# Last expert pair by column blocks with an early scatter, and filler products ahead of the mask

## The chip, the cores and the metric

The kernel runs on one core of a Trainium2 chip. The metric is the device time of one execution in microseconds. One program computes the whole model; no collective is in it.

## The reference

A trunk of two residual layers on 256 tokens of width 2048, all float32. Layer 0 mixes tokens with a chunkwise mLSTM, layer 1 with latent attention (MLA). Behind each mixer stands a mixture of 16 experts in 4 groups, of which each token uses 2:

```python
for i in range(DEPTH):
    x = x + mixer_i(rmsnorm(x, norm_mix[i]))
    x = x + moe_ffn(rmsnorm(x, norm_ffn[i]), router_w, router_b, w_gate[i], w_up[i], w_down[i])

def moe_ffn(xn, ...):
    scores = sigmoid(xt @ router_w); sel = scores + router_b
    # best group of 4 experts, its best 2, their scores normalised to gates
    hg, hu = xt @ w_gate[e], xt @ w_up[e]          # 2048 -> 512 for each expert e
    a = silu(hg) * hu * gates
    y = sum over e of a[e] @ w_down[e]             # 512 -> 2048
```

An expert's three matrices have 12 MB, so those of a layer are 192 units of 1 MB. Each is read once.

## The kernel before

The order of the work is written out by hand for each engine, with semaphores between them. The program in order of time: mLSTM projections and heads with its output projection (to about 437 us), router, experts of layer 0 (to about 910), MLA (to about 1273), router, experts of layer 1.

**Loads.** SP issues all weight loads. In an expert stage a load is mostly a double unit of 2 MB into one of 8 double slots (DOUBLE, OVD, WIDED), and it waits (`room`) until PE has used what lay there, counted by the semaphore `unit_used`. The down weights' last two double units of the last pair (`HALVES = 4`) come as four loads of 1 MB, first the two first halves (k = 0, experts e = 0 and 1), then the two second halves (L489).

**Start of an expert stage.** PE ends the router's logits (L657), VectorE and ScalarE make from them a mask of the two experts of each token (L1771 to L1795), and PE waits for it in `route` (L836): three products (L837 to L839) give each token its position in its expert's list of up to 64 tokens, two (L841, L842) the counts. VectorE makes a selection matrix (L1823), and `gather` (L868) takes the normalised tokens XN, which ScalarE writes meanwhile in eight pieces (L1322), to the experts' slots in four column groups. The first pair gathers two groups, multiplies with the first half of the weights (L908), gathers two more and goes on.

**A pair** (function `pair` of PE) handles two experts side by side in the two halves of TensorE's columns, 64 slots each: gate and up products (L908), in whose gaps the scatter of the pair before stands; transposes of A and of the selection (L922 to L927); the down products (L940). These run over c, the four blocks of the contraction (512 = 4 x 128), and inside it over d, the four column blocks of the result, which lie in PSUM banks 4 to 7. Blocks c = 0 and 1 need the first double unit of down weights of each expert, c = 2 and 3 the second; in the last pair c = 2 needs the first halves and c = 3 the second halves of it. After c = 3, d each column block is read by ScalarE (Y_hi, L1338) and by VectorE (Y_lo, L1873).

**Scatter and add.** `scatter` (L880, L881) brings column block d of the two experts' results back to the two token blocks t, two products for each, into banks 2 and 3. `add_block` of VectorE (L1837) adds them to X. The scatter of block d + 1 waits until the add of block d has read its bank. Behind the last pair of a layer the four scatters stand behind all down products, and VectorE's four `add_block` behind all four Y_lo (semaphore `x_final`).

**Behind layer 0** `turn_final` (L599) transposes each finished column block for the attention layer, VectorE multiplies it with the norm's gains (`final_turned`, L1520), ScalarE (L1308) and POOL (L566) split it into a high and a low part, and PE's first attention products (`token_unit`, L627) need these and the high (ScalarE, L1149) and the low part (VectorE, L1510) of the weights. Behind layer 1 SP stores each column block of X (L540).

Of the kernel before, what the change touches and what calls it, by code (L numbers as in the profile page):

```python
# [136 lines left out]
TURNS = ("h", "n2")  # L137
N2_BANKS = (0, 4, 6, 2)

# [38 lines left out]
def trunk(nc, w, out):  # L178
# [8 lines left out]
    with ctx:  # L187
# [405 lines left out]
        def _(pe):  # L593
# [256 lines left out]
            def experts(l, base):  # L850
# [21 lines left out]
                def scatter(m, j, d, final=False):  # L872

                    pe.wait_ge(sem(m + "y_low"), 4 * j + d + 1)
                    for t in range(NT):
                        if d > 0 and final:
                            pe.wait_ge(sem("x_final"), 8 * l + 2 * d + t - 1)
                        elif d > 0:
                            pe.wait_ge(sem(m + "x_added"), 8 * (j - l) + 2 * d + t - 1)
                        pe.matmul(PS[:, 2 + t, :], SCT[:, t * P:(t + 1) * P], YH[:, d, :], start=True, stop=False)  # L880
                        pe.matmul(PS[:, 2 + t, :], SCT[:, t * P:(t + 1) * P], YL[:, d, :], start=False, stop=True)\  # L881
                            .then_inc(sem(m + "scattered"), 1)

                def pair(m, j, g, following, arrived, slot, consumed, whole, prev, first=False):
# [46 lines left out]

                    for c in range(FC):
                        units = [16 + 4 * (c // 2) + 2 * e + c % 2 for e in range(2)]
                        for n in units:
                            arrived(n)
                        for d in range(4):
                            if c == 0 and d == 2:
                                pe.wait_ge(sem(m + "sct_ready"), j + 1)
                            for e in range(2):
                                last = pe.matmul(PS[64 * e:64 * e + 64, 4 + d, :], m_["AT"][:, c, 64 * e:64 * e + 64],  # L940
                                                 slot(units[e])[:, d, :], start=(c == 0), stop=(c == FC - 1))
                                if d == 3:
                                    finished(last, units[e])
# [52 lines left out]
            for n in range(4):  # L996
                token_unit(S_CKV + n, (0, 1), XTP, UNIT_K * n, n == 0, n == 3, False, chunks("n2", n), True)
                if n < 2:
                    turn_final(n + 2)
            pe.wait_ge(sem("few_lo"), 2)  # L1000
            for k in range(DC):
                last = three(PS[0:ROPE, 4, 0:SEQ], [v[:, k, :] for v in WKRP], (XTH[:, k, :], XTL[:, k, :]),
                             k == 0, k == DC - 1)
# [68 lines left out]
            for i in range(N_PAIR):  # L1072
# [6 lines left out]
                if i == 0:  # L1079
                    pe.wait_ge(sem("krope_copied"), 1)  # L1080
                    for t in range(NT):
                        last = pe.transpose(PS[:, 4, t * ROPE:(t + 1) * ROPE], KRX[:, t * P:(t + 1) * P],
                                            IDENT[0:ROPE, 0:ROPE])
# [49 lines left out]
        def _(act):  # L1133
# [246 lines left out]
            for t in range(NT):  # L1380
                act.activation(b_["CKV"][:, t, :], PS[:, t, :], ACT.Copy, scale=RST[:, t:t + 1]).then_inc(sem("ckv_copied"), 1)
            high(S_PAIRS + 1)
            act.wait_ge(sem("krope_done"), 1)
            act.activation(KRX, PS[0:ROPE, 4, 0:SEQ], ACT.Copy).then_inc(sem("krope_copied"), 1)
            act.wait_ge(sem("ckv_means"), 1)
            act.activation(SSQ[:, 4:6], SSQ[:, 2:4], ACT.Sqrt).then_inc(sem("ckv_roots"), 1)
            act.wait_ge(sem("krope_done"), 2)
            for t in range(NT):
                last = act.activation(b_["KR"][:, t, :], PS[:, 4, t * ROPE:(t + 1) * ROPE], ACT.Copy, scale=RST[:, t:t + 1])
            last.then_inc(sem("krope_copied"), 1)  # L1390
# [104 lines left out]
        def _(dve):  # L1495
# [319 lines left out]
            def experts(l):  # L1815
# [17 lines left out]
                def add_block(m, j, d, counted):  # L1833
                    for t in range(NT):
                        dve.wait_ge(sem(m + "scattered"), 8 * j + 2 * d + t + 1)
                        xs = X[:, t, d * UNIT_C:(d + 1) * UNIT_C]
                        tt(xs, PS[:, 2 + t, :], xs, ALU.add).then_inc(sem(counted), 1)  # L1837

# [10 lines left out]

                def pair(m, j, following, ahead, products, prev, i, first):  # L1850
                    select_again(m, j, i, first)
# [31 lines left out]
                def main(i, j, following, ahead, prev):  # L1883
                    pair(m, j, following, lambda: ahead, lambda n: dve.wait_ge(sem("unit_used"), base + PAIR_UNITS * i + n), prev, i, 0)

# [259 lines left out]
```

## Time and profile before

| | |
|---|---|
| median of 3 runs | 1754.29 us (1751.32 to 1754.47) |
| the profiled execution | 1753.88 us |
| its span | 1752.1 us, mean granted clock 0.99 |
| PE busy | 1689.9 us (96%) |
| VectorE, ScalarE, POOL busy | 756.4, 493.7, 51.8 us |
| DMA | 531.70 MB, 303 GB/s over the span |

A profile comes from one execution. Times in it are in microseconds from the span's start. "Idle before" is the time for which an engine did nothing ahead of an instruction, with what ended it. PEclk is the granted clock of TensorE as a share of 2.4 GHz, so 0.50 is 1.2 GHz. The chain of waits is followed back from the last instruction. An f32 product stands in it as two records. The DMA share is that of the core's 16 DMA engines.

### The profile page before, as it was taken

To read this page: it belongs to the slowest core of one execution; us is meant where nothing else is said; L and a number is where in the kernel's file an instruction comes from. 1 tells how busy PE (TensorE), PEld (TensorE's weight loads), DVE (VectorE), ACT (ScalarE), POOL (GpSimd) and SP (SyncE) were. 2 spreads that over 40 slices of the span, in tenths; PEclk is the share of its full clock that TensorE was granted. 3 is DMA by queue.
4 is the path that set the end of the run, shared out by engine and by line. 5 is a ranking of instruction groups with operands and counts; after the bars stand their busy time and mean duration, and the time that the engine had idled before them with its cause. 6 is when DMAs were issued, how large, how long until landed. Compare 5 with 4: busy or idle time off the path is not lost.

```text
span 1752.1 us, 21040 instructions
## 1 busy us (share of the span) xinstructions
PE 1689.9 (96%) x8834; PEld 1095.5 (63%) x8834; DVE 756.4 (43%) x1276; ACT 493.7 (28%) x649; POOL 51.8 (3%) x32
## 2 busy tenths in 40 slices
PE   7999999999899999999999999999989999999998
PEld 7998777788444443443458999988854443444343
DVE  4775577754222222222246777784422222222222
ACT  4435456542200000000034565664330000000000
POOL 2000000000000000000021000010000000000000
PEclk9999999999899999999999999999989999999999
DMA  9655534464999999999994545454589999999996
GB/s 312 204 184 168 188 123 129 136 211 149 380 420 428 427 428 428 427 427 428 427 373 156 161 133 156 145 173 161 195 341 420 428 428 428 426 428 428 426 428 280
DMA packets 102376, 531.70 MB, mean 303 GB/s; under 512 B 11764, under 2 KB 28680, under 8 KB 76936
## 3 DMA queue, kind: packets, MB, share of 16 engines
q1 hardware_dynamic: 101904, 530.16, 77.0%
q8 instruction: 74, 1.21, 0.3%
q10 hardware_dynamic: 344, 0.13, 0.0%
q14 instruction: 22, 0.18, 0.0%
q0 software_dynamic: 32, 0.02, 0.0%
HBM read 528.19 MB, written 2.10 MB: 303 GB/s over the span
## 4 chain that ended last, share of the span: by engine, by line
PE 85%; DMA 10%; DVE 2%; ACT 1%; issue 1%; ACTq 0%; DVEq 0%; SPq 0%
PE PS L627 31%; PE PS L908 19%; PE PS L940 13%; PE PS L868 7%; PE PS L710 5%; DMA DOUBLE<-in_moe_w_up 5%; DMA OVD<-in_moe_w_up 3%; DMA OVD<-in_moe_w_down 2%; PE PS L880 2%; PE PS L881 1%; PE PS L795 1%; PE PS L1043 1%; PE PS L1069 1%; PE PS L657 1%; ACT AREA L1330 1%
## 5 line engine op out<-in xcount | busy, mean ns | idle before, releaser
L908 PE MATMUL PS<-DOUBLE,AREA 128*64 128x512 f32 x1280 | 350.0, 604 | 22.1 <-DMA DOUBLE<-in_moe_w_up 8.2
L1510 DVE TENSOR_TENSOR LO<-ring,HI 128x2048 fp32r<-128x2048 f32 (+1 forms) x124 | 267.2, 2155 | 182.0 <-ACT HI L1149 181.8
L1149 ACT ACTIVATE HI<-ring 128x2048 fp32r<-128x2048 f32 (+1 forms) x124 | 223.7, 1805 | 275.6 <-PE PS L627 228.5
L908 PEld LDWEIGHTS PS<-DOUBLE,AREA 128*64 128x64 f32 x1280 | 107.5, 139 | 236.4 <-issue 228.9
L908 PE MATMUL PS<-OVD,AREA 128*64 128x512 f32 x512 | 229.6, 596 | 0.0
L1837 DVE TENSOR_TENSOR X<-PS,X 128x512 f32<-128x512 f32 x128 | 82.4, 686 | 331.1 <-PE PS L881 331.1
L940 PE MATMUL PS<-DOUBLE,AREA 128*64 128x512 f32 x640 | 168.2, 594 | 2.1 <-DMA OVD<-in_moe_w_down 0.2
L627 PE MATMUL PS<-HI,XTH 128*128 128x512 f32 (+1 forms) x672 | 159.7, 379 | 1.5 <-ACT HI L1149 1.5
L627 PE MATMUL PS<-LO,XTH 128*128 128x512 f32 (+1 forms) x672 | 152.8, 369 | 0.0
L627 PE MATMUL PS<-HI,XTL 128*128 128x512 f32 (+1 forms) x672 | 152.5, 368 | 0.0
L627 PEld LDWEIGHTS PS<-HI,XTL 128*128 128x128 f32 x672 | 122.9, 188 | 16.4
L627 PEld LDWEIGHTS PS<-LO,XTH 128*128 128x128 f32 x672 | 122.8, 188 | 16.5 <-DVE LO L1510 0.3
L627 PEld LDWEIGHTS PS<-HI,XTH 128*128 128x128 f32 x672 | 121.0, 188 | 18.6 <-ACT HI L1149 2.1
L868 PEld LDWEIGHTS PS<-AREA,XN 128*128 128x128 f32 x1024 | 121.3, 199 | 13.9 <-issue 13.0
L1873 DVE SCALAR_TENSOR_TENSOR Y_lo<-PS,AREA,Y_hi 128x512 fp32r<-128x512 f32 x64 | 48.1, 751 | 189.4 <-ACT Y_hi L1338 183.8
L868 PE MATMUL PS<-AREA,XN 128*128 128x128 f32 x1024 | 124.7, 284 | 0.8 <-DVE AREA L1823 0.8
L1328 ACT ACTIVATE AREA<-PS 128x512 f32<-128x512 f32 x16 | 9.6, 597 | 410.7 <-PE PS L908 410.7
L908 PE MATMUL PS<-WIDED,AREA 128*64 128x512 f32 x256 | 115.6, 595 | 5.5 <-DMA OVD<-in_moe_w_up 5.5
L940 PEld LDWEIGHTS PS<-DOUBLE,AREA 128*64 128x64 f32 x640 | 52.9, 137 | 103.6 <-issue 100.1
L940 PE MATMUL PS<-OVD,AREA 128*64 128x512 f32 x256 | 111.7, 594 | 0.0
L1338 ACT ACTIVATE Y_hi<-PS,AREA 128x512 fp32r<-128x512 f32 x64 | 44.0, 688 | 192.5 <-PE PS L940 192.5
L1846 DVE TENSOR_TENSOR AREA<-PS,VFF 128x512 f32<-128x512 f32 x64 | 44.3, 692 | 102.0 <-PE PS L868 102.0
(291 smaller groups left out, 1828.8 us busy)
## 6 DMA issues: line engine op xcount, KB each, us to landing
DOUBLE<-in_moe_w_gate SPq DMA_DIRECT2D x48, 2048.0 KB, 20.4
DOUBLE<-in_moe_w_down SPq DMA_DIRECT2D x40, 2048.0 KB, 21.8
DOUBLE<-in_moe_w_up SPq DMA_DIRECT2D x32, 2048.0 KB, 23.3
ring<-in_a_w_in SPq DMA_DIRECT2D x48, 1024.0 KB, 5.1
OVD<-in_moe_w_gate SPq DMA_DIRECT2D x16, 2048.0 KB, 24.8
WIDED<-in_moe_w_up SPq DMA_DIRECT2D x16, 2048.0 KB, 22.5
OVD<-in_moe_w_up SPq DMA_DIRECT2D x16, 2048.0 KB, 27.1
OVD<-in_moe_w_down SPq DMA_DIRECT2D x14, 2048.0 KB, 27.3
```

What stands on the lines that cost most here:

```text
L627: mm = pe.matmul(PS[:, banks[t], 0:n], lhs(k0 + kk, t)[part], weights[:, kk, 0:n], start=first and kk == 0 and p == 0, stop=last and kk == ...
L710: last = pe.matmul(PS[:, 4 * (b % 2) + ch, 0:SEQ], weights[:, kk, ch * P:(ch + 1) * P], tokens[:, k, :], start=k == 0 and p == 0, stop=k = ...
L868: last = pe.matmul(PS[:, bank, k * P:(k + 1) * P], XN[:, t, c * P:(c + 1) * P], m_["SEL"][:, t, :], start=(t == 0), stop=(t == NT - 1))
L880: pe.matmul(PS[:, 2 + t, :], SCT[:, t * P:(t + 1) * P], YH[:, d, :], start=True, stop=False)
L908: last = pe.matmul(PS[64 * e:64 * e + 64, up, :], m_["XG"][:, c, 64 * e:64 * e + 64], slot(units[e])[:, kk, :], start=(c == 0), stop=(c == ...
L940: last = pe.matmul(PS[64 * e:64 * e + 64, 4 + d, :], m_["AT"][:, c, 64 * e:64 * e + 64], slot(units[e])[:, d, :], start=(c == 0), stop=(c ...
L1149: act.activation(HI[s % 2][:, :, 0:n], ring[PLACE[u]][:, :, 0:n], ACT.Copy).then_inc(sem("hi_ready"), 1)
L1338: act.activation(YH[:, d, :], PS[:, 4 + d, :], ACT.Copy, scale=m_["GS"])\
L1510: tt(LO[PLACE[u]][:, :, 0:n], ring[PLACE[u]][:, :, 0:n], HI[s % 2][:, :, 0:n], ALU.subtract)\
L1837: tt(xs, PS[:, 2 + t, :], xs, ALU.add).then_inc(sem(counted), 1)
L1846: tt(m_["XG"][:, 4 * g:4 * g + 4, :], ps4(2 + g % 2), VFF[:, l, 4 * g:4 * g + 4].unsqueeze(2).broadcast_to([P, 4, P]), ALU.mult)\
L1873: stt(YL[:, d, :], PS[:, 4 + d, :], m_["GS"], YH[:, d, :], ALU.mult, ALU.subtract)\
```

## The change

1. `route` of both layers begins with four f32 products of 512 columns (ONES by X) into bank 0, ahead of the wait for the mask. Nobody reads their result.
2. In the last pair of each layer the down products of c = 0 and 1 stand as before. Those of c = 2 and 3 go by column block: both for d = 0, both for d = 1, and so on. The waits for the first and second halves of the last double units stand together ahead of them.
3. Scatter of column block 0 stands between the down products of d = 2 and d = 3, and VectorE's add of block 0 ahead of its Y_lo 3.
4. The final scatters use banks 2 and 3 for d = 0 and 2, and banks 0 and 1 for d = 1 and 3 (`FINAL_BANKS`); block d waits for the adds of block d - 2.
5. `turn_final` uses banks 4, 6, 2, 0 in this order (before 0, 4, 6, 2), the first attention unit's results go to banks 4 and 5 (before 0 and 1), and the rope part of the keys to bank 0 (before 4).

```diff
+            def keep_on(bank, *columns):
+                for n in columns:
+                    pe.matmul(PS[:, bank, 0:n], ONES, X[:, 0, 0:n], start=True, stop=True)
+
             def route(l):
+                keep_on(0, 512, 512, 512, 512)
                 pe.wait_ge(sem("mask_ready"), l + 1)
...
                     for t in range(NT):
-                        if d > 0 and final:
-                            pe.wait_ge(sem("x_final"), 8 * l + 2 * d + t - 1)
-                        elif d > 0:
+                        bank = FINAL_BANKS[d] + t if final else 2 + t
+                        if d > 1 and final:
+                            pe.wait_ge(sem("x_final"), 8 * l + 2 * d + t - 3)
+                        elif d > 0 and not final:
                             pe.wait_ge(sem(m + "x_added"), 8 * (j - l) + 2 * d + t - 1)
...
+                    ending = whole and not following
+                    for c in range(2 if ending else FC):
+                        down_arrived(c)
                         for d in range(4):
                             if c == 0 and d == 2:
                                 pe.wait_ge(sem(m + "sct_ready"), j + 1)
+                            last = down(c, d)
                             if c == FC - 1 and d < 3:
                                 last.then_inc(sem(m + "y_done"), 1)
+                    if ending:
+                        down_arrived(2)
+                        down_arrived(3)
+                        for d in range(4):
+                            down(2, d)
+                            last = down(3, d)
+                            if d < 3:
+                                last.then_inc(sem(m + "y_done"), 1)
+                            if d == 2:
+                                scatter(m, j, 0, True)
...
-                for d in range(4):
+                for d in range(1, 4):
                     scatter(m, pair_turn(l, PAIRS - 1), d, True)
...
                     for d in range(4):
+                        if d == 3 and last_one:
+                            add_block(m, j, 0, "x_final")
                         dve.wait_ge(sem(m + "y_ready"), 4 * j + d + 1)
...
-                for d in range(4):
+                for d in range(1, 4):
                     add_block(m, pair_turn(l, PAIRS - 1), d, "x_final")
```

PE ahead of the mask products, first the kernel before, then the changed one (L657 and L658 are the logits, MK is the mask, the words in brackets are the semaphores waited for):

```order
L657 MATMUL PS<-RW,XT_110 128x16 [waits x_columns]
L657 MATMUL PS<-RW,XT_110 128x16 x3
L837 MATMUL PS<-MK,TRI_R 128x16 [waits mask_ready]
L838 MATMUL PS<-MK,ONE_R 128x16
L839 MATMUL PS<-MK,TRI_R 128x16
```

```order
L658 MATMUL PS<-RW,XT_110 128x16 [waits x_columns]
L658 MATMUL PS<-RW,XT_110 128x16 x3
L839 MATMUL PS<-X,CON 128x512 x4
L845 MATMUL PS<-MK,TRI_R 128x16 [waits mask_ready]
L846 MATMUL PS<-MK,ONE_R 128x16
L847 MATMUL PS<-MK,TRI_R 128x16
```

The four filler products (CON holds ONES) stand between the logits and the wait for the mask.

PE at the end of layer 1, the second half of the down products. Before, its first rows and those where c = 3 begins (unit_loaded_12 and 14 are the first halves, 13 and 15 the second halves):

```order
L940 MATMUL PS<-DOUBLE_111,AREA 64x512
L940 MATMUL PS<-OVD_60,AREA 64x512
L940 MATMUL PS<-WIDED,AREA 64x512 [waits unit_loaded_14,unit_loaded_12]
L940 MATMUL PS<-OVD_59,AREA 64x512
L940 MATMUL PS<-WIDED,AREA 64x512
L940 MATMUL PS<-OVD_59,AREA 64x512
L940 MATMUL PS<-WIDED,AREA 64x512
L940 MATMUL PS<-OVD_59,AREA 64x512
L940 MATMUL PS<-WIDED,AREA 64x512
L940 MATMUL PS<-OVD_59,AREA 64x512
L940 MATMUL PS<-WIDED,AREA 64x512 [waits unit_loaded_15,unit_loaded_13]
L940 MATMUL PS<-OVD_59,AREA 64x512
```

The changed kernel at the same place:

```order
L944 MATMUL PS<-DOUBLE_111,AREA 64x512
L944 MATMUL PS<-OVD_60,AREA 64x512
L944 MATMUL PS<-WIDED,AREA 64x512 [waits unit_loaded_13,unit_loaded_15,unit_loaded_14,unit_loaded_12]
L944 MATMUL PS<-OVD_59,AREA 64x512
L944 MATMUL PS<-WIDED,AREA 64x512
L944 MATMUL PS<-OVD_59,AREA 64x512
```

Before, the second halves are waited for eight rows (four column blocks) later than the first halves; now all four loads are waited for ahead of the first product of the second half.

VectorE at the end of layer 1, before and now:

```order
L1870 CAST SCT<-PS 128x256
L1873 SCALAR_TENSOR_TENSOR Y_lo<-PS,AREA,Y_hi 128x512 [waits m_y_ready] x4
L1837 TENSOR_TENSOR X<-PS,X 128x512 [waits m_scattered] x8
```

```order
L1898 CAST SCT<-PS 128x256
L1903 SCALAR_TENSOR_TENSOR Y_lo<-PS,AREA,Y_hi 128x512 [waits m_y_ready] x3
L1865 TENSOR_TENSOR X<-PS,X 128x512 [waits m_scattered] x2
L1903 SCALAR_TENSOR_TENSOR Y_lo<-PS,AREA,Y_hi 128x512 [waits m_y_ready]
L1865 TENSOR_TENSOR X<-PS,X 128x512 [waits m_scattered] x6
```

Two of the eight adds now stand ahead of the last Y_lo.

## Rows read from the trace of the kernel before

**Rows 1.** Busy time by stretch: us, each engine's busy us (x), PEclk, DMA share, GB/s.

```profile
672.00:889.00 217.00, 203.03 (x1006) 87.54 (x1002) 51.70 (x88) 14.23 (x23) 0.00 (x0) 0.99 1.01 427
911.00:1268.00 357.00, 354.59 (x1913) 316.44 (x1911) 240.68 (x406) 193.18 (x279) 28.10 (x11) 1.00 0.51 166
```

**Rows 2.** The chain that ended last, layer 1's end: start us, us, what.

```profile
1688.15 27.87 DMA DOUBLE<-in_moe_w_up
...
1716.15 8.75 PE PS L908 x32
...
1727.47 14.00 PE PS L940 x64
...
1742.22 0.75 DVE Y_lo L1873
```

**Rows 3.** Timeline of VectorE, the last two adds: start us, us, what, [idle before].

```profile
1747.61 1.29 DVE L1837 TENSOR_TENSOR X<-PS,X 128x512 f32<-128x512 f32 x2 [0.29 <-PE PS L881]
```

**Rows 4.** Start of both expert stages: PE and ScalarE timelines, then the chain.

```profile
445.70 0.38 PE L837 MATMUL PS<-MK,TRI_R 128*128 128x16 f32 x1 [4.08 <-DVE MK L1795]
...
442.69 9.13 ACT L1322 ACTIVATE XN<-X,SSQ 128x512 f32<-128x512 f32 x8
...
1281.82 0.38 PE L837 MATMUL PS<-MK,TRI_R 128*128 128x16 f32 x1 [4.40 <-DVE MK L1795]
...
447.32 6.59 PE PS L868 x32
453.91 13.88 PE PS L908 x64
467.79 3.77 PE PS L868 x32
...
1283.44 6.66 PE PS L868 x32
```

**Rows 5.** Busy time by stretch, the clock at layer 0's start.

```profile
444.00:452.00 8.00, 5.91 (x27) 5.82 (x28) 3.70 (x17) 7.82 (x7) 0.00 (x0) 0.50 1.00 429
454.00:456.00 2.00, 2.00 (x10) 0.61 (x10) 0.64 (x1) 0.00 (x0) 0.00 (x0) 1.00 0.99 410
```

**Rows 6.** Busy time by stretch, where the load slots are full.

```profile
458.00:464.00 6.00, 6.00 (x30) 2.01 (x28) 0.00 (x0) 0.00 (x0) 0.00 (x0) 1.00 0.63 208
1294.00:1300.00 6.00, 6.00 (x32) 2.00 (x30) 0.00 (x0) 0.00 (x0) 0.00 (x0) 1.00 0.54 180
```

**Rows 7.** The last half loads (L489), SP's timeline and times to landing, both layers.

```profile
869.80 0.43 SPq L489 DMA_DIRECT2D OVD<-in_moe_w_down  x1
...
DMA to landing us min/median/max: 23.3/26.7/30.0
...
1705.41 0.43 SPq L489 DMA_DIRECT2D OVD<-in_moe_w_down  x1
...
DMA to landing us min/median/max: 24.2/27.3/30.3
```

**Rows 8.** The chain: a scatter between two groups of products.

```profile
512.42 7.02 PE PS L908 x32
...
519.87 0.23 PE PS L881
...
520.56 7.02 PE PS L908 x32
```

**Rows 9.** End of layer 0: the chain, then VectorE's timeline.

```profile
889.48 14.11 PE PS L940 x64
...
910.17 2.48 DVE L1510 TENSOR_TENSOR LO<-ring,HI 128x2048 fp32r<-128x2048 f32 x1
```

**Rows 10.** PE timeline: products behind an idle time, with the idle time before them.

```profile
794.46 5.33 PE L908 MATMUL PS<-DOUBLE,AREA 128*64 128x512 f32 x16 [2.57 <-DVEq L1906]
...
869.88 3.65 PE L908 MATMUL PS<-DOUBLE,AREA 128*64 128x512 f32 x16 [1.42 <-DMA DOUBLE<-in_moe_w_gate]
...
1716.15 2.83 PE L908 MATMUL PS<-DOUBLE,AREA 128*64 128x512 f32 x6 [2.28 <-DMA DOUBLE<-in_moe_w_up]
```

More of the change, by code:

```diff
@@ L137 @@
 TURNS = ("h", "n2")
-N2_BANKS = (0, 4, 6, 2)
+N2_BANKS = (4, 6, 2, 0)
+FINAL_BANKS = (2, 0, 2, 0)
 OVER_PE = (("gathered", 4 * OVER_PAIRS + 4), ("a_turned", OVER_PAIRS), ("sel_turned", OVER_PAIRS), ("y_done", 3 * OVER_PAIRS),
@@ L875, in scatter @@
                     for t in range(NT):
-                        if d > 0 and final:
-                            pe.wait_ge(sem("x_final"), 8 * l + 2 * d + t - 1)
-                        elif d > 0:
+                        bank = FINAL_BANKS[d] + t if final else 2 + t
+                        if d > 1 and final:
+                            pe.wait_ge(sem("x_final"), 8 * l + 2 * d + t - 3)
+                        elif d > 0 and not final:
                             pe.wait_ge(sem(m + "x_added"), 8 * (j - l) + 2 * d + t - 1)
-                        pe.matmul(PS[:, 2 + t, :], SCT[:, t * P:(t + 1) * P], YH[:, d, :], start=True, stop=False)
-                        pe.matmul(PS[:, 2 + t, :], SCT[:, t * P:(t + 1) * P], YL[:, d, :], start=False, stop=True)\
+                        pe.matmul(PS[:, bank, :], SCT[:, t * P:(t + 1) * P], YH[:, d, :], start=True, stop=False)
+                        pe.matmul(PS[:, bank, :], SCT[:, t * P:(t + 1) * P], YL[:, d, :], start=False, stop=True)\
                             .then_inc(sem(m + "scattered"), 1)
@@ L930, in pair, with down, down_arrived @@
                     pe.wait_ge(sem(m + "at_ready"), j + 1)
-                    for c in range(FC):
+                    def down(c, d):
                         units = [16 + 4 * (c // 2) + 2 * e + c % 2 for e in range(2)]
-                        for n in units:
-                            arrived(n)
+                        for e in range(2):
+                            last = pe.matmul(PS[64 * e:64 * e + 64, 4 + d, :], m_["AT"][:, c, 64 * e:64 * e + 64],
+                                             slot(units[e])[:, d, :], start=(c == 0), stop=(c == FC - 1))
+                            if d == 3:
+                                finished(last, units[e])
+                        return last
+                    def down_arrived(c):
+                        for e in range(2):
+                            arrived(16 + 4 * (c // 2) + 2 * e + c % 2)
+                    ending = whole and not following
+                    for c in range(2 if ending else FC):
+                        down_arrived(c)
                         for d in range(4):
@@ L938, in pair @@
                                 pe.wait_ge(sem(m + "sct_ready"), j + 1)
[L939 to L943, printed above, removed]
+                            last = down(c, d)
                             if c == FC - 1 and d < 3:
                                 last.then_inc(sem(m + "y_done"), 1)
+                    if ending:
[8 more added lines that the diff above has]
+                                scatter(m, j, 0, True)
                     if following:
@@ L996, in _ @@
             for n in range(4):
-                token_unit(S_CKV + n, (0, 1), XTP, UNIT_K * n, n == 0, n == 3, False, chunks("n2", n), True)
+                token_unit(S_CKV + n, (4, 5), XTP, UNIT_K * n, n == 0, n == 3, False, chunks("n2", n), True)
                 if n < 2:
@@ L1001, in _ @@
             for k in range(DC):
-                last = three(PS[0:ROPE, 4, 0:SEQ], [v[:, k, :] for v in WKRP], (XTH[:, k, :], XTL[:, k, :]),
+                last = three(PS[0:ROPE, 0, 0:SEQ], [v[:, k, :] for v in WKRP], (XTH[:, k, :], XTL[:, k, :]),
                              k == 0, k == DC - 1)
@@ L1081, in _ @@
                     for t in range(NT):
-                        last = pe.transpose(PS[:, 4, t * ROPE:(t + 1) * ROPE], KRX[:, t * P:(t + 1) * P],
+                        last = pe.transpose(PS[:, 0, t * ROPE:(t + 1) * ROPE], KRX[:, t * P:(t + 1) * P],
                                             IDENT[0:ROPE, 0:ROPE])
@@ L1380, in _ @@
             for t in range(NT):
-                act.activation(b_["CKV"][:, t, :], PS[:, t, :], ACT.Copy, scale=RST[:, t:t + 1]).then_inc(sem("ckv_copied"), 1)
+                act.activation(b_["CKV"][:, t, :], PS[:, 4 + t, :], ACT.Copy, scale=RST[:, t:t + 1]).then_inc(sem("ckv_copied"), 1)
             high(S_PAIRS + 1)
             act.wait_ge(sem("krope_done"), 1)
-            act.activation(KRX, PS[0:ROPE, 4, 0:SEQ], ACT.Copy).then_inc(sem("krope_copied"), 1)
+            act.activation(KRX, PS[0:ROPE, 0, 0:SEQ], ACT.Copy).then_inc(sem("krope_copied"), 1)
             act.wait_ge(sem("ckv_means"), 1)
@@ L1388, in _ @@
             for t in range(NT):
-                last = act.activation(b_["KR"][:, t, :], PS[:, 4, t * ROPE:(t + 1) * ROPE], ACT.Copy, scale=RST[:, t:t + 1])
+                last = act.activation(b_["KR"][:, t, :], PS[:, 0, t * ROPE:(t + 1) * ROPE], ACT.Copy, scale=RST[:, t:t + 1])
             last.then_inc(sem("krope_copied"), 1)
@@ L1836, in add_block @@
                         xs = X[:, t, d * UNIT_C:(d + 1) * UNIT_C]
-                        tt(xs, PS[:, 2 + t, :], xs, ALU.add).then_inc(sem(counted), 1)
+                        bank = FINAL_BANKS[d] + t if counted == "x_final" else 2 + t
+                        tt(xs, PS[:, bank, :], xs, ALU.add).then_inc(sem(counted), 1)
                 def added(m, j):
@@ L1848, in gathered, with pair @@
                             .then_inc(sem(m + "xg_ready"), 1)
-                def pair(m, j, following, ahead, products, prev, i, first):
+                def pair(m, j, following, ahead, products, prev, i, first, last_one=False):
                     select_again(m, j, i, first)
@@ L1883, in main @@
                 def main(i, j, following, ahead, prev):
-                    pair(m, j, following, lambda: ahead, lambda n: dve.wait_ge(sem("unit_used"), base + PAIR_UNITS * i + n), prev, i, 0)
+                    pair(m, j, following, lambda: ahead, lambda n: dve.wait_ge(sem("unit_used"), base + PAIR_UNITS * i + n), prev, i, 0, not following)
                 main(0, pair_turn(l, 0), True, gather_turn(l, 1), False)
```

## Prediction

> **What bounds the kernel now.** The profiled execution took 1753.88 us with a span of 1752.1; the median of the runs shown is 1754.29, 0.4 us above it. The sum below is made against the profiled one; about 0.2% (3.5 us) is what a measurement of this kernel can tell from no change.
>
> I read the stretches first [rows 1]. In the second half of each expert stage the DMA engines are fully busy at 427 GB/s while PE has some 14 us of idle in 217. So weights streaming in set the end of both expert stages, and PE only adds what it does after the last weights. In the attention stage between them PE is busy 354.6 of 357 us: a delay handed to it passes through.
>
> Next the chain that ended last, at the end of layer 1 [rows 2]: it comes from a landing (the last up weights, until 1716.02), then 8.75 us of products, the 14.00 us of down products, a Y_hi and a Y_lo of 1.5 us together (to 1742.97). Behind it two adds to X at a time take 1.29 us and are preceded by 0.29 us of waiting for a scatter, a period of 1.57, until 1748.90 [rows 3]: scatter and add take turns on one pair of banks. The store follows.
>
> Then the start of an expert stage [rows 4]. PE is idle 4.08 us (layer 0) and 4.40 us (layer 1) for the mask. The granted clock is 0.50, that is 1.2 GHz, from 444 to 452 and back at 2.4 GHz at 454 [rows 5]. The first 32 gather products therefore take 6.59 and 6.66 us where the same number takes 3.77 at full clock: 2.8 and 2.9 us. This would be hidden behind the DMA, but the slots are full at that point: the next load is issued when PE has finished with the first double slot, and for six us DMA moves 208 and 180 GB/s in place of 427 [rows 6]. That is (427 - 208) x 6 / 427 = 3.1 us of lost streaming in layer 0 and 3.5 in layer 1, which a DMA-bound stage never gets back.
>
> **Part 1: four filler products, twice.** Each is an f32 product of 512 columns. The nearest row is 64 records (32 half-width products, 16 pairs side by side) in 13.88 us: 0.87 us each; from the 128-column gather (3.77 us for 16 products, times four for the columns) it would be 0.94. Four take 3.5 to 3.8 us at full clock. They start when the logits end (445.70 - 4.08 = 441.62; in layer 1 1281.82 - 4.40 = 1277.42) and end at 445.1 to 445.4 and 1280.9 to 1281.2, ahead of the mask products (445.70, 1281.82) [rows 4]. Queued behind them on PE are only those mask products. The gather then runs at full clock, if these products keep it granted or bring it back before 447.3. It is not limited elsewhere at once: ScalarE writes XN in eight pieces of 1.14 us from 442.69 [rows 4], so the second column group, after four of them, is ready at 447.3, as the first group starts.
>
> PE gains 2.8 and 2.9 us there. The next load is issued that much sooner, and the stream, which lost 3.1 and 3.5, gains at most 2.9. Bounds: nothing to 2.9 in each layer. I take 2.5 and 2.7, since a load's rate also rises only over some 2 us after an idle queue. **-5.2 us.**
>
> **Part 2: the second half of the down products in column blocks.** The first half takes 8 of 16 steps of 14.00 / 16 = 0.875 us, so 7.0 us. Before, the third quarter waited for the first two half loads and the fourth for the last two. Now both waits stand ahead of the first column block, after 7.0 us in place of 10.5. The last half load was issued at 869.80 and 1705.41 and took 30.0 and 30.3 us: it lands at 899.8 and 1735.7 [rows 7]. DMA sets this, so it moves with part 1 but not with part 2.
>
> Layer 1: down starts at 1727.47, the first half ends at 1734.5, PE waits 1.3 us, restarts at about 1735.9. Then 7.0 us of products and one scatter between them. Between products a scatter costs what lies from 512.42 + 7.02 = 519.44 to 520.56, 1.12 us [rows 8]. The last product ends at 1744.0 (1741.5 before). Y_hi and Y_lo take 1.5 us (to 1745.5). Block 0 is then already added, in the time VectorE waits for the last Y_hi, and with two pairs of banks the other three blocks run at VectorE's own 1.29 us: 1749.4 against 1748.9 (1747.61 + 1.29) [rows 3]. So +0.5, and +0.1 as the stores, 1.57 us apart before, come 1.29 apart: **+0.6 us.** Without the wait it would be 0.9 us faster: from the last product to the last add 7.4 us fall to 5.4, less 1.1 for the scatter.
>
> By the Trainium skill, "TensorEngine Tiling (Array Packing)", Key Properties, a change of tiling mode drains TensorE. The scatter is full width and stands between half-width products, so it changes mode twice. By the rate of scatter products in a row (0.23 [rows 8]) the term would be 0.93, by the row with both changes in it 1.12, which stands in the sum; the rule costs 0.2 us per layer and the trace agrees with it.
>
> Layer 0: down starts at 889.48, the first half ends at 896.5, the last half load lands at 899.8. PE waits **3.4 us**. Then 8.1 us: 908.1 in place of 889.48 + 14.11 = 903.6 [rows 9]. Y_lo 3 ends at 909.6. VectorE then does three double operations (add 1, the turned block, add 2) where it did four: 3 x 1.28, so the low half of the first attention weights starts at 913.4 in place of 910.17 [rows 9]. PE's second group of attention products needs that low half. **+3.2 us**, and PE, busy through the attention stage [rows 1], absorbs none of it.
>
> The clock after that wait: an idle time of 2.57 us ahead of 794.46 was followed by slow products, 16 records in 5.33 us in place of 3.65 [rows 10]: **+1.7 us.** Bounds: nothing to 1.7. I take 1.7, since 3.4 us is longer than that row's idle time.
>
> The new PSUM banks move no work; the attention stage's waits for them are for operations that it waited for anyway. I cost them at nothing.
>
> Sum: 1753.88 - 5.2 + 3.2 + 1.7 + 0.6 = **1754.2 us**: what the fillers give is spent on the wait for the last loads in layer 0. Chance 0.42.
>
> **Rivals.**
> (a) The wait is there, the clock stays: 1.7 less, **1752.5**, 0.2. For it: an idle time of 1.42 us ahead of 869.88 left the clock alone (the 16 records behind it took 3.65) [rows 10]. Against it: 2.28 us ahead of 1716.15 did not, and the 32 records there took 8.75 in place of 7.02 [rows 2, 8]. Where the limit falls isn't seen. The Trainium skill, "TensorE: Matmul & The Clock Gate", Part 1, says that the monitor behind the clock runs free of the program; by it the same wait may cost nothing in one run and 1.7 in the next, and no run so far shows this wait twice.
> (b) Layer 0's delay is absorbed in the attention stage, where ScalarE and VectorE have waits of their own: -5.2 + 0.6, **1749.3**, 0.15. Against it: PE's 354.6 of 357 us.
> (c) Slower: the fillers themselves run at 1.2 GHz. Ahead of them PE has had little but the router's 16-column products, and the clock was down by 444 [rows 5]. Four fillers then take 7 us, end at 448.6 and 1284.4, and hold back the mask products by 2.9 and 2.5. The gather still gains its 2.8, so the fillers gain 0 and 0.3: 1753.88 - 0.3 + 5.5 = **1759.1**, 0.15. It decides from the point where the fillers end more than some 2 us after the mask; half of them cold ends 1 us late and only costs 1 us of the gain.
> (d) The change doesn't do what it says: the fillers leave the clock at half in the gather too. They are then 2.9 and 2.5 us late for nothing: 1753.88 + 5.4 + 5.5 = **1764.8**, 0.03.
> The last 0.05 is for what I have not thought of.
>
> **How the numbers follow.** Faster needs 1750.8 or less: (b), and a little of (a): 0.19. Slower needs 1757.8: (c) and (d): 0.18. Within: 0.63. The range takes in the forecast with its bounds (gains of 4.5 to 5.7 in part 1, 0 to 1.7 of clock), most of (a), and the nearer half of (b) and (c): 1749.8 to 1757.8.
>
> **What would show it.** First gather products near 3.8 us in both layers and the clock at 1.0 at 446:448; the load after them issued 2.8 us sooner relative to the mask. In layer 0 a PE wait of about 3.4 us for a down load, followed by products at half clock; in layer 1 one of about 1.3. X adds of blocks 1 to 3 without gaps of 0.28 between them. From the first gather product to the last down landing some 2.5 us less. If PE has no wait for the last loads, the steps of part 2 are wrong, and the time is 1 us better in layer 1 and over 3 in layer 0; if fillers end after the mask, (c) is at work.

## The result, and the profile of the changed kernel

| | before | changed |
|---|---|---|
| median of 20 runs | 1752.36 us (1749.13 to 1754.51) | 1756.1 us (1752.7 to 1759.46) |
| ratio | | 1.0021, 95% interval 1.0014 to 1.0028 |
| profiled execution | 1753.88 us | 1757.23 us |
| its span | 1752.1 us | 1755.6 us, mean granted clock 0.994 |
| PE busy | 1689.9 us | 1694.0 us |
| VectorE, ScalarE, POOL busy | 756.4, 493.7, 51.8 us | 756.1, 493.2, 51.8 us |

The changed kernel is slower by 3.7 us (2.5 to 4.9). The forecast was no change. The time, 1756.1, lies in the range, but the median of before fell to 1752.36 with more runs: the profile against which the sum was made was 1.5 us above it.

The start of the expert stages first. PE's timeline of the changed kernel, both layers (start us, us, instructions, idle before with what ended it):

```profile
441.38 3.68 PE L839 MATMUL PS<-X,CON 128*128 128x512 f32 x8
445.62 0.28 PE L845 MATMUL PS<-MK,TRI_R 128*128 128x16 f32 x1 [0.55 <-DVE MK L1822]
447.18 3.84 PE L876 MATMUL PS<-AREA,XN 128*128 128x128 f32 x32 [0.84 <-DVE AREA L1850]
...
1279.43 3.68 PE L839 MATMUL PS<-X,CON 128*128 128x512 f32 x8
1283.98 0.28 PE L845 MATMUL PS<-MK,TRI_R 128*128 128x16 f32 x1 [0.87 <-DVE MK L1822]
1285.55 5.46 PE L876 MATMUL PS<-AREA,XN 128*128 128x128 f32 x32 [0.84 <-DVE AREA L1850]
```

The four fillers take 3.68 us and end 0.55 and 0.87 us ahead of the mask, at full clock. In layer 0 the gather takes 3.84 us where it took 6.59 [rows 4]. In layer 1 it takes 5.46 (6.66 before): 1.2 us less and not 2.8, so more than half of what the fillers should give is missing. The stretches agree (each engine's busy us, PEclk, DMA share, GB/s):

```profile
458.00:464.00 6.00, 6.00 (x32) 2.00 (x30) 0.00 (x0) 0.00 (x0) 0.00 (x0) 1.00 0.95 363
1284.00:1290.00 6.00, 5.16 (x30) 5.07 (x31) 2.25 (x9) 6.00 (x6) 0.00 (x0) 0.72 1.01 434
1294.00:1300.00 6.00, 6.00 (x30) 2.01 (x28) 0.00 (x0) 0.00 (x0) 0.00 (x0) 1.00 0.84 303
```

Where the load slots are full, DMA moved 208 and 180 GB/s [rows 6]; now it moves 363 and 303. The second of these stretches does not stand at the same place of its stage, since the mask of layer 1 comes 2.16 us later. Over sixty us at the same place (from 440 in layer 0, from 1277 before and 1279.16 now in layer 1) the rate rises from 403 to 417 GB/s in layer 0, and from 404 to 412 in layer 1. The granted clock of 1284 to 1290 is 0.72: it is 1.00 until 1285 and 0.50 from 1286 to 1289, so most of that gather ran at 1.2 GHz.

Then the last pair. PE's timeline shows three idle times: ahead of the second half of the down products in each layer, and in the middle layer 1's last up products.

```profile
896.96 1.08 PE L944 MATMUL PS<-WIDED,AREA 128*64 128x512 f32 x1 [2.88 <-DMA OVD<-in_moe_w_down]
...
1717.40 7.09 PE L917 MATMUL PS<-DOUBLE,AREA 128*64 128x512 f32 x32 [2.33 <-DMA DOUBLE<-in_moe_w_up]
...
1737.07 1.09 PE L944 MATMUL PS<-WIDED,AREA 128*64 128x512 f32 x1 [2.80 <-DMA OVD<-in_moe_w_down]
```

PE waits 2.88 and 2.80 us for a down load. In the kernel before, its longest wait for one in these two pairs was 0.25 us. The first record behind the wait takes 1.08 us, where the first one of the down products, at full clock, takes 0.61, and the stretches show the clock:

```profile
897.00:900.00 3.00, 3.00 (x8) 1.07 (x10) 0.00 (x0) 0.00 (x0) 0.00 (x0) 0.50 1.05 386
...
1737.00:1738.00 1.00, 0.93 (x4) 0.37 (x6) 0.00 (x0) 0.00 (x0) 0.00 (x0) 0.50 0.00 0
```

The chain of waits tells what each layer's end hangs on. Layer 0:

```profile
869.00 27.83 DMA OVD<-in_moe_w_down
...
896.96 6.97 PE PS L944 x24
...
905.06 1.92 PE PS L944 x8
...
907.73 0.75 DVE Y_lo L1903
908.48 1.20 DVE X L1865 x2
909.67 1.20 DVE AREA L1547 x2
910.87 1.20 DVE X L1865 x2
912.06 2.70 DVE LO L1537
...
914.81 3.97 PE PS L628 x16
```

Layer 1:

```profile
1706.62 30.32 DMA OVD<-in_moe_w_down
...
1737.07 6.75 PE PS L944 x24
...
1744.94 1.92 PE PS L944 x8
...
1747.61 0.75 DVE Y_lo L1903
1748.36 2.39 DVE X L1865 x4
...
1751.35 0.60 DVE X L1865
```

Both now begin with the landing of the last half load. Where the 3.5 us of span come from:

- Layer 0: PE's first products with the low half of the attention weights start at 914.81, before at 912.71: +2.1. This passes through the attention stage whole: the mask of layer 1 comes at 1283.98, before at 1281.82 [rows 4], +2.16.
- Layer 1, from mask to last add: 1751.95 - 1283.98 = 467.97; before 1748.90 - 1281.82 = 467.08: +0.9.
- From the last add to the end of the span: 3.65 us, before 3.2: +0.45.

### The profile page after: what moved, and what is told of

Same layout as the page of the kernel before. It is cut to its first block, busy times and chain, and to the rows that moved or that the text cites. A ratio compares the mean times of both kernels' runs of the same rounds, so it can differ in the third digit from the quotient of the medians.

```text
span 1755.6 us, 21070 instructions
## 1 busy us (share of the span) xinstructions
PE 1694.0 (96%) x8850; PEld 1094.4 (62%) x8850; DVE 756.1 (43%) x1276; ACT 493.2 (28%) x649; POOL 51.8 (3%) x32
## 4 chain that ended last, share of the span: by engine, by line
PE 79%; DMA 16%; DVE 2%; ACT 1%; issue 1%; SPq 0%; ACTq 0%; DVEq 0%
PE PS L628 30%; PE PS L917 15%; PE PS L944 11%; DMA OVD<-in_moe_w_up 6%; PE PS L876 6%; DMA DOUBLE<-in_moe_w_up 6%; PE PS L711 5%; DMA OVD<-in_moe_w_down 3%; PE PS L889 1%; PE PS L796 1%; PE PS L890 1%; PE PS L1070 1%; PE PS L1096 1%; PE PS L658 1%; PE PS L1075 0%
## 5 line engine op out<-in xcount | busy, mean ns | idle before, releaser
L917 PE MATMUL PS<-OVD,AREA 128*64 128x512 f32 x512 | 229.8, 596 | 0.0
L628 PE MATMUL PS<-HI,XTH 128*128 128x512 f32 (+1 forms) x672 | 159.9, 379 | 1.8 <-ACT HI L1176 1.5
L628 PE MATMUL PS<-LO,XTH 128*128 128x512 f32 (+1 forms) x672 | 152.8, 369 | 0.8 <-DVE LO L1537 0.8
L628 PE MATMUL PS<-HI,XTL 128*128 128x512 f32 (+1 forms) x672 | 152.5, 368 | 0.0
L628 PEld LDWEIGHTS PS<-LO,XTH 128*128 128x128 f32 x672 | 122.8, 188 | 17.5 <-DVE LO L1537 1.3
L628 PEld LDWEIGHTS PS<-HI,XTL 128*128 128x128 f32 x672 | 122.9, 188 | 16.4
L628 PEld LDWEIGHTS PS<-HI,XTH 128*128 128x128 f32 x672 | 120.9, 188 | 19.2 <-ACT HI L1176 2.1
L876 PEld LDWEIGHTS PS<-AREA,XN 128*128 128x128 f32 x1024 | 117.3, 194 | 14.8 <-issue 13.0
L876 PE MATMUL PS<-AREA,XN 128*128 128x128 f32 x1024 | 120.7, 279 | 1.7 <-DVE AREA L1850 1.7
L944 PE MATMUL PS<-OVD,AREA 128*64 128x512 f32 x256 | 115.4, 607 | 0.0
```

The lines of the kernel that those rows point to most:

```text
L628: mm = pe.matmul(PS[:, banks[t], 0:n], lhs(k0 + kk, t)[part], weights[:, kk, 0:n], start=first and kk == 0 and p == 0, stop=last and kk == ...
L876: last = pe.matmul(PS[:, bank, k * P:(k + 1) * P], XN[:, t, c * P:(c + 1) * P], m_["SEL"][:, t, :], start=(t == 0), stop=(t == NT - 1))
L917: last = pe.matmul(PS[64 * e:64 * e + 64, up, :], m_["XG"][:, c, 64 * e:64 * e + 64], slot(units[e])[:, kk, :], start=(c == 0), stop=(c == ...
```

## The experiments

Two names for short: the "early wait" is that both pairs of half loads are waited for ahead of the second half; the "exit" of layer 1 is the time from the first down product of the last pair to the end of the last add. It was 1748.90 - 1727.47 = 21.43 us before and is 1751.95 - 1727.19 = 24.76 in the changed kernel. For layer 0 the same is counted to the first low products (L627, L628): 23.23 and 27.81. All medians below stand beside runs of the kernel before on the same chip.

### 1. Each half of the change alone

The fillers alone:

```diff
 def route(l):
+    keep_on(0, 512, 512, 512, 512)
     pe.wait_ge(sem("mask_ready"), l + 1)
```

> The kernel before with the four filler products in both layers and nothing else. Theory A (the slowdown is all in the last pair; the fillers gain 2.9 us where the clock is up for the gather and 1.2 where it falls between mask and gather, as in layer 1 of the changed kernel's trace): 1.2 to 5.8 us under before, likeliest 4, and both ends of the expert stages as before, with no wait for a half load. Rival B (the fillers do not shorten the stage, the DMA gives nothing back): within 1 us of before. Rival C (the fillers cost, the ending is innocent): 2 us or more over before.

Measured: 1748.0 us against 1752.22, ratio 0.9978 (0.9969 to 0.9987): **4.2 us faster**. Both gathers run at full clock, in PE's timeline:

```profile
447.17 3.84 PE L872 MATMUL PS<-AREA,XN 128*128 128x128 f32 x32 [0.84 <-DVE AREA L1827]
...
1280.96 3.84 PE L872 MATMUL PS<-AREA,XN 128*128 128x128 f32 x32 [0.59 <-DVE AREA L1827]
```

PE saves 2.8 us in each. From gather to first down product layer 0 takes 886.97 - 447.17 = 439.80 us, before 889.48 - 447.32 = 442.16: 2.4 less. Layer 1, from gather to the last up products, takes 1.9 less (430.85 and 432.71). Rivals B and C fall.

In layer 1 the fillers of this run did not stay at full clock themselves. PE's timeline and the stretch show it:

```profile
1274.53 5.38 PE L836 MATMUL PS<-X,CON 128*128 128x512 f32 x8
...
1276.00:1278.00 2.00, 2.00 (x3) 0.72 (x3) 1.50 (x7) 2.00 (x4) 0.00 (x0) 0.50 0.97 418
```

They took 5.38 us in place of 3.68, and the gather started 6.43 us after the first of them, where it is 6.12 in the changed kernel's layer 1: 0.3 us of the gain is lost. This is rival (c) of the prediction in its half form.

The rest of the change, without fillers:

> The changed kernel without its fillers. Theory A: the early wait for the last half loads costs about 3 us of idle PE and 1.5 of slow clock in layer 0 and 1.5 to 4 in layer 1, so 6 to 9 us over before, PE idle ahead of the second half of the down products 3.4 us in layer 0. Rival B (fillers worth nothing): 3 to 4 over before, as the changed kernel. Rival C: no slower than before.

Measured: 1759.05 us, ratio 1.0041 (1.0027 to 1.0054): **6.8 us slower**. Its idle times:

```profile
899.50 0.69 PE L943 MATMUL PS<-WIDED,AREA 128*64 128x512 f32 x1 [3.31 <-DMA OVD<-in_moe_w_down]
...
1740.97 0.61 PE L943 MATMUL PS<-WIDED,AREA 128*64 128x512 f32 x1 [2.77 <-DMA OVD<-in_moe_w_down]
```

So the change is two of opposite sign, and the second is the larger: -4.2 + 6.8 = +2.6, against +3.7 measured for both, within what the intervals allow.

### 2. Is it the wait, or what came with it?

The early wait alone, in the kernel before: no fillers, column blocks or new banks.

```diff
 for c in range(FC):
     units = [16 + 4 * (c // 2) + 2 * e + c % 2 for e in range(2)]
-    for n in units:
+    early = whole and not following
+    for n in [] if early and c == 3 else units + [20 + 2 * e + 1 for e in range(2)] if early and c == 2 else units:
         arrived(n)
```

> The kernel before with one thing changed: in the last pair of each layer the wait for the second half loads stands ahead of c = 2 in place of c = 3. No fillers, no column blocks, no new banks. Theory A (the wait alone makes the slowdown): PE idle 3 to 3.4 us ahead of c = 2 in layer 0 and 1.3 to 2.8 in layer 1, mostly with slow products behind, 5 to 8 us over before. Rival (the wait needs the column blocks or the scatter to cost): under 3 us over before.

Measured: 1759.4 us against 1751.93, ratio 1.0041 (1.0027 to 1.0054): **7.5 us slower**, as much as the whole second part. In each layer the two second half loads, waited for eight products (3.5 us) sooner, make the slowdown:

```profile
898.23 0.81 PE L941 MATMUL PS<-WIDED,AREA 128*64 128x512 f32 x1 [4.04 <-DMA OVD<-in_moe_w_down]
...
1738.41 1.08 PE L941 MATMUL PS<-WIDED,AREA 128*64 128x512 f32 x1 [2.80 <-DMA OVD<-in_moe_w_down]
```

Next the changed kernel with only the early wait taken out, by going back to the old order over c:

```diff
 down_arrived(2)
-down_arrived(3)
 for d in range(4):
     down(2, d)
+down_arrived(3)
+for d in range(4):
     last = down(3, d)
```

> The changed kernel with its second half in the old order over c: all four column blocks of c = 2 behind the wait for the first half loads, then the wait for the second half loads and c = 3, with scatter 0 between its column blocks 2 and 3. Only the early wait is gone; fillers, early scatter and two pairs of banks stay. Theory A: no idle time over 0.6 us ahead of c = 3, no slow clock there; 3 to 6 us under before, 7 to 10 under the changed kernel. Rival B (the cost is the scatter between products and the new banks, not the wait): within 1 us of the changed kernel.

Measured: 1747.43 us, ratio 0.9974 (0.9965 to 0.9983): 4.8 us faster than before, and 8.2 (by the ratios) to 8.7 (by the medians) faster than the changed kernel. In its chain the products from the first one to the scatter stand in one piece, in both layers:

```profile
887.82 13.10 PE PS L944 x60
...
900.92 0.43 PE PS L889
```

```profile
1721.77 13.10 PE PS L944 x60
1734.86 0.43 PE PS L889
```

60 of the 64 records in 13.10 us without a gap. Layer 1's exit is 20.37 us.

Last, column blocks as in the changed kernel, but with the last loads cut to fit: a half load brings two column blocks of both k.

```diff
-sp.dma_start(DOUBLE[PLACE[u + 2 * e]][:, k, :, :].rearrange("p k c -> p (k c)"), half(srcs[-2 + e], k))\
+cols = slice(1024 * k, 1024 * k + 1024)
+sp.dma_start(DOUBLE[PLACE[u + 2 * e]][:, :, 2 * k:2 * k + 2, :].rearrange("p k d c -> p k (d c)"),
+             srcs[-2 + e].rearrange("p (k c) -> p k c", k=2)[:, :, cols])\
...
 down_arrived(2)
-down_arrived(3)
 for d in range(4):
+    if d == 2:
+        down_arrived(3)
     down(2, d)
     last = down(3, d)
```

> The changed kernel with the last four loads cut as its products use them: each half load brings two column blocks of both rows k (c = 2 and 3) in place of all columns of one k, so column blocks 0 and 1 need the first two half loads and 2 and 3 the second two; the wait for the latter stands ahead of column block 2, 10.5 us after the first down product. Column blocks, early scatter and banks as in the changed kernel. Theory A (column blocks cost only because the loads are cut the other way): no idle time over 0.6 us ahead of the second half, 20.4 us from the first down product to the last add in layer 1 (24.8 in the changed kernel), as fast as the run with the late wait, 3.5 to 6 us under before. Rival (column blocks or runs of 4 KB in the loads cost by themselves): 2 us or more slower than that.

Measured: 1746.49 us against 1751.9, ratio 0.9973 (0.9962 to 0.9983). Its chain in layer 1:

```profile
1719.89 12.24 PE PS L946 x56
1732.13 0.43 PE PS L891
```

No gap again, and an exit of 1740.26 - 1719.89 = 20.37 us. The order by column blocks costs nothing and gains nothing; it cost because a column block needs both k, and the loads came one k at a time. The rival about 4 KB runs falls too, at this resolution.

### 3. What the clock has of it

The wait stays, but PE has three more fillers in it:

```diff
+keep_on(0, 512, 512, 512)
 down_arrived(2)
 down_arrived(3)
```

> The changed kernel with three more filler products (2.8 us at full clock) ahead of the wait for the last half loads, so that the wait stays and only PE's idle time in it goes. Theory A (part of the cost is the clock, half speed for some 3 us behind an idle wait of 2.8): the first products behind the wait run at full clock in both layers, 1.4 to 1.7 us less in each, so 2.5 to 3.5 us under the changed kernel, about level with before. Rival D (the clock falls whatever PE does in the wait, or the slow products hide behind something): no difference to the changed kernel. If the half loads have landed before the fillers end, they cost instead what they overlap, up to 0.3 us.

Measured: 1752.97 us, ratio 1.0004 (0.9995 to 1.0013), 3.1 us under the changed kernel. PE's timeline in both layers:

```profile
893.83 2.84 PE L839 MATMUL PS<-X,CON 128*128 128x512 f32 x6
896.79 0.61 PE L944 MATMUL PS<-WIDED,AREA 128*64 128x512 f32 x1
...
1731.50 2.84 PE L839 MATMUL PS<-X,CON 128*128 128x512 f32 x6
1734.37 0.61 PE L944 MATMUL PS<-WIDED,AREA 128*64 128x512 f32 x1
```

The second half of layer 1 takes 1742.80 - 1734.37 = 8.43 us where the changed kernel takes 1746.86 - 1737.07 = 9.79: 1.36 us of clock. In layer 0 it is 905.22 - 896.79 = 8.43 against 906.98 - 896.96 = 10.02: 1.59. So of the some 8 us of the early wait, about 3 are the clock behind it in two layers. The rest is the wait itself: this run is 5.5 us slower than the one with the late wait (1752.97 and 1747.43).

### 4. Early scatter, banks, VectorE's order

The late wait, but all four scatters and adds behind the down products again, with the two pairs of banks kept:

```diff
-if d == 2:
-    scatter(m, j, 0, True)
...
-for d in range(1, 4):
+for d in range(4):
     scatter(m, pair_turn(l, PAIRS - 1), d, True)
...
-if d == 3 and last_one:
-    add_block(m, j, 0, "x_final")
```

> The run with the late wait (fillers, two pairs of banks, old order over c), but without the early scatter and the early add: all four scatters behind the down products, the four adds behind Y_lo 3. By the rows an early scatter costs 1.12 us between products and saves one add of 1.2 at the end, so theory: within 0.5 us of the run with the early scatter, at the end of layer 1 within 0.3 (20.4 us from the first down product to the last add). Rival (the early scatter is what gains): 1 us or more slower than that run.

Measured: 1747.76 us, ratio 0.9974 (0.9965 to 0.9983), as with the early scatter. VectorE's eight adds of layer 1 stand without a gap:

```profile
1739.30 4.87 DVE L1864 TENSOR_TENSOR X<-PS,X 128x512 f32<-128x512 f32 x8
```

The exit is 1744.17 - 1723.88 = 20.29 us (20.37 with the early scatter, 21.43 before): the 1.1 us come from the second pair of banks alone. In layer 0 it is 22.71 us where the early scatter has 23.11. A scatter of 1.12 us on PE buys an add of 1.2 on VectorE.

Then, with the early scatter again, layer 0's low half ahead of the add of block 2 on VectorE:

```diff
 if l == 0 and d == 1:
     final_turned(0)
+    low(S_CKV)
 if l == 0 and d == 2:
-    low(S_CKV)
     final_turned(1)
```

> The run with the late wait, but VectorE makes the low half of the first attention weights ahead of the add of block 2 in layer 0 in place of behind it. PE waited 0.83 us for it. Theory: that wait goes, the first low products start 0.8 us sooner after the down products (22.3 us from the first of them in place of 23.1), the time falls by 0.8. Rival: the turned block 1, now later on VectorE, is waited for instead, no difference.

Measured: 1744.94 us (5 runs), ratio 0.9962 (0.9948 to 0.9975). In the trace PE's low products follow the high ones at once:

```profile
909.22 2.08 PE L628 MATMUL PS<-HI,XTH 128*128 128x512 f32 x8 [0.24 <-ACT XTH L1336]
911.14 1.99 PE L628 MATMUL PS<-LO,XTH 128*128 128x512 f32 x8
```

Layer 0's exit is 22.13 us, 1.0 less than the 23.11 with the old order. The medians do not part this run from the one with the late wait: the intervals (0.9948 to 0.9975 and 0.9965 to 0.9983) overlap.

### 5. Fillers in other idle times, and the parts that gained

Fillers ahead of the last up weights, in that kernel:

```diff
 units = [8 * q + 4 * up + 2 * e + k for e in range(2)]
+if whole and not following and q == 1 and up == 1 and k == 0:
+    keep_on(5, 512, 256)
```

> The run before this one with two more filler products (512 and 256 columns, 1.4 us) in the last pair of each layer, in the idle time ahead of the last up weights (2.3 us in the trace before, 1.4 to 3.0 elsewhere). Theory: the slow clock behind that wait (8.7 in place of 7.1 us for 32 records, in some executions) is seen no more, on average 0.5 to 1 us less and fewer slow executions. Rival: the clock there is not set by that idle time, or the weights' landing comes before the fillers end: no difference or up to 0.4 us more.

Measured: 1746.3 us, ratio 0.9966 (0.9955 to 0.9977): nothing that shows beside the run before. Its profile has no slow stretch in an expert stage. But layer 1's last up products ran at full clock in the run above too (7.09 us), so the two profiles tell nothing of the worth of this piece: inconclusive, and left out of the last two.

The parts that gained: the run without the early scatter, and on VectorE the same move of `low(S_CKV)` as above, with no other edit:

> The parts that gained, together: fillers, two pairs of banks behind the down products without the early scatter, and the low half of the first attention weights ahead of the add of block 2 in layer 0. By the traces of its parts 1745 to 1747 where before has 1752; level with the run that had the early scatter and the same order on VectorE. Rival (without the early scatter that order gains nothing): 0.8 us more.

Measured: 1746.48 us, ratio 0.9966 (0.9954 to 0.9978). Layer 0's exit is 907.01 - 885.23 = 21.78 us, the shortest so far. Level with the run that had the early scatter; the rival of 0.8 us more in layer 0 falls by the trace.

And in that kernel one filler more:

```diff
     .then_inc(sem("counts"), 1)
+keep_on(0, 384)
```

> The run before this one with one more filler product (384 columns, 0.7 us) in each layer between the counts and the gather, where PE is idle 0.6 to 0.8 us. Theory: whether the gather starts at full clock hangs on the idle time and thin products between fillers and gather (in two of seven profiles with fillers layer 1's took 5.4 us in place of 3.8); with less idle time both gathers take 3.84 us and the median falls by up to 0.5 us. Rival (this idle time does not matter): no difference.

Measured: 1745.29 us (5 runs), ratio 0.9965 (0.9952 to 0.9979). Its fillers and gathers:

```profile
439.61 5.38 PE L839 MATMUL PS<-X,CON 128*128 128x512 f32 x8
...
446.03 3.84 PE L877 MATMUL PS<-AREA,XN 128*128 128x128 f32 x32
...
1272.45 5.38 PE L839 MATMUL PS<-X,CON 128*128 128x512 f32 x8
...
1278.87 3.84 PE L877 MATMUL PS<-AREA,XN 128*128 128x128 f32 x32
```

Both gathers at full clock, but this profile does not test the theory: the four fillers ahead were slow in both layers, and behind such fillers the gather ran at full clock without the extra one too. Nor does the median part it from the run before. With these two, ten profiles of kernels with fillers give twenty starts of an expert stage. In six the fillers took 5.38 us and the gather behind them 3.84 (layer 0 in four profiles, layer 1 in two). In three, all of layer 1, the fillers took 3.68 and the gather 5.46, 5.39 or 5.40. In the other eleven both ran at full clock. Slow fillers start the gather 0.6 us later in layer 0 (6.4 us after the first filler, not 5.8) and 0.3 in layer 1.

**The best version** is any of the last four; they are 5.4 to 7.0 us under before and 9 to 11 under the changed kernel, and these runs cannot rank them. Nor do the intervals part any of them from the run with fillers alone (0.9978, 0.9969 to 0.9987): what the second pair of banks (1.1 us) and VectorE's order (1.0 us) gain stands on the traces.

## Why the prediction was wrong, step by step

The mechanisms were right: fillers gain by the clock, and the early wait costs. That the two nearly cancel was wrong, because two terms of layer 1 were: the gain of the fillers was taken as 2.7 us and was 0.9, and the slow products behind layer 1's wait, 1.4 us, were put at nothing without a reason. By the traces, changed against before (1751.95 - 1736.94 = 15.0 us from landing to last add, before 1748.90 - 1735.7 = 13.2):

| term | forecast | measured |
|---|---|---|
| layer 0: fillers, wait, clock, to the first low products | -2.5 + 3.2 + 1.7 = +2.4 | +2.1 |
| layer 1: fillers, at the last landing | -2.7 | -0.9 |
| layer 1: from that landing to the last add | +0.5 | +1.8, of it 1.4 slow clock |
| layer 1: stores | +0.1 | +0.45 |
| all | +0.3 | +3.5 |

**Part 1, layer 0** was right: fillers of 3.68 us (3.5 to 3.8 forecast), gather at 3.84, down start 2.5 us sooner (887.00 for 889.48). **Layer 1 is the first step that failed.** The landing of the last half load against the mask is 1736.94 - 1283.98 = 452.96, before 1735.7 - 1281.82 = 453.9. The step took 2.7 on the condition that the fillers "keep it granted"; in this profile the clock fell all the same, as the gather began: between fillers and gather PE had 0.87 and 0.84 us of idle with 16-column products between. The same two gaps stood ahead of layer 1's gathers at full clock in other runs, so why it fell here stays open. The step's own lower bound was nothing, but the sum took a value near the upper end twice. Even at full clock 2.7 was too much: with fillers alone layer 1 got 1.9 us from gather to the last up products, and the two layers together gave 4.2, not 5.2.

**Part 2, layer 1 is the second.** "PE waits 1.3 us" was read from a down start at 1727.47 and carried no clock term. That down start was late because the last up products of that profile ran slow, 8.75 us [rows 2], the very row quoted against rival (a). At full clock they take 7.09, down starts 9.75 us ahead of the last landing and not 8.24, and the wait is 2.80 us (1.3 + 1.5), as long as layer 0's and, like it, followed by slow products. In the profile of before those slow up products set the end; in the changed kernel the landing sets it, and to run faster ahead of it brings nothing. The step should have priced the wait from the landing back to a down start at full clock.

**Layer 0's wait** was 3.4 us in the forecast and 2.88 in the trace, with the clock at 0.50 behind it (1.6 us, forecast 1.7); 3.31 and 4.04 in the runs without fillers. The delay went through the attention stage whole (+2.1 at its start, +2.16 at its end), so rival (b) is out.

**The scatter** between products was priced at 1.12 us, and that is what it took (1743.82 to 1744.94). The gapless adds were priced at 1.29 a block and took 1.2. The exit of 20.37 us without the wait is 1.06 under before, 0.9 forecast. **The stores** took 0.45 us more behind the last add, not 0.1; the same shows in every run with gapless adds (3.6 to 4.1 us from the last add to the end, and 3.2 to 3.3 in the three kernels with gaps between them).

Rival (a), the clock stays behind the wait, did not hold: it fell in both layers. Rivals (c) and (d) did not happen in this profile: the fillers ended ahead of the mask. In six of the twenty starts of a stage above, (c) happened in the half form that the prediction names, and cost 0.3 to 0.6 us, not 1. The slowdown came from a case that the prediction had no rival for: slow products behind the waits of both layers, and layer 1's gather partly slow. The chance of slower, 0.18, hung on the fillers alone.

The median of before was taken as 0.4 us from the profile; with 20 runs it is 1.5 under it. A profile with a slow stretch in it that the change removes or makes harmless is a poor base, and this one had such a stretch 36 us from the end. An estimate from its rows: with the last up products at 7.09 us and not 8.75 it would have ended 1.66 us sooner, at 1752.2. The last half load, landed at 1735.7, would still have come before c = 3, then due at 1727.47 + 10.5 - 1.66 = 1736.3.

## What to carry to other kernels

When products are put into another order, ask which piece of the last load each of them needs: a block order and the cut of the loads go together, and either the wait must stay where the piece is needed or the load must be cut like the products. Price a new wait from the landing, at full clock, and add the slow products behind it in every place where the wait stands, not in one. Split a change that joins a gain and a cost before judging it: here the fillers were worth 4.2 us and were spent by a wait that moved 3.5 us.

## What was not expected of the hardware

The length of PE's idle time does not decide whether slow products follow. Ahead of the last up products of layer 1, 2.28 us of idle were followed by 8.75 us (before), 2.33 by 7.09 (changed); ahead of the second half of layer 1's down products 2.80 us were followed by 1.08 us a record and 2.77 by 0.61 (the changed kernel without fillers). The clock can even fall with PE at work: in the run with fillers alone it was 0.50 from 1276 to 1278, in the middle of layer 1's fillers, and ahead of them PE had done the logits' 16-column products with no gap over 0.35 us. The Trainium skill, "TensorE: Matmul & The Clock Gate", Part 1, says that the monitor runs free of the program, so that the same kernel differs from run to run. No kernel here was profiled twice, but the traces of different kernels agree with it: the same instructions at the same place, with nearly the same waits ahead of them, differ by 1.4 to 1.7 us.

The landing of the last load comes long after the stream has thinned out. DMA by stretches at the end of layer 1 in the changed kernel:

```profile
1730.00:1732.00 2.00, 2.00 (x12) 0.76 (x10) 0.00 (x0) 0.00 (x0) 0.00 (x0) 1.00 0.96 401
1732.00:1733.00 1.00, 1.00 (x8) 0.45 (x6) 0.00 (x0) 0.00 (x0) 0.00 (x0) 1.00 0.57 238
...
1735.00:1736.00 1.00, 0.00 (x0) 0.00 (x0) 0.00 (x0) 0.00 (x0) 0.00 (x0) 1.00 0.10 41
1736.00:1737.00 1.00, 0.00 (x0) 0.00 (x0) 0.00 (x0) 0.00 (x0) 0.00 (x0) 0.74 0.02 8
```

PE waited for 2.80 us while DMA moved under a tenth of its rate for the last two of them. So a wait at the very end of a stream is not priced by bytes over its full rate. A share of 0.10 of 16 engines means fewer than two busy on average; which ones lag, and why, these views do not show. Whether a smaller last load would land sooner was not tried.
